# Hybrid decoder layer on one core: the values of head group A projected token-major ahead of attention, and pairs of 12 units instead of 16

## The reference

```
def dilated_attention(q, k, v, slopes):            # group A
    for window, d in ((128, 1), (512, 4), (2048, 16)):
        num, m, sm = banded_parts(every d-th token of q, k, v, slopes, window // d, d)
    w = [exp(m_i - max of m)]                      # the three branches are merged
    return sum(num_i * w_i) / sum(s_i * w_i)
def swa_sink_attention(q, k, v, slopes, sinks):    # group B: window of 128, a sink in the denominator
    return (num * c) / (s * c + exp(sink - m2))

mix = concat(rmsnorm(out_a, g_a), rmsnorm(out_b, g_b))
x = x + mix @ w_out
h = rmsnorm(x, ffn_norm)
x = x + (silu(h @ w_gate) * (h @ w_up)) @ w_down   # inner width 5632
return rmsnorm(x, final_norm)
```

## Time and profile before

| | |
|---|---|
| time, median of 3 runs | 1996.04 us (1995.95 to 1996.41) |
| time of the profiled execution | 1995.92 us |
| span of its trace | 1994.1 us |
| PE busy | 1984.3 us, 10380 matmuls |
| DVE, ACT, POOL busy | 1612.9, 1091.5, 145.6 us |
| one pair with attention (359.4 to 416.5 us of the span) | 57.1 us: DVE 37.0, ACT 31.7, POOL 14.1 us busy |

### The profile page before, as it was taken

How to read it: one execution, slowest core, us unless ns; L and a number is a source line. 1 busy time by engine, 2 the same in 40 slices (tenths; PEclk the granted TensorE clock), 3 DMA queues, 4 the chain that set the end, 5 groups by cost and what they waited for, 6 DMA issues and landing times.

```text
span 1994.1 us, 30321 instructions
## 1 busy us (share of the span) xinstructions
PE 1984.3 (100%) x10380; PEld 1703.7 (85%) x10380; DVE 1612.9 (81%) x2319; ACT 1091.5 (55%) x2001; POOL 145.6 (7%) x241
## 2 busy tenths in 40 slices
PE   9999999999999999999999999999999999999998
PEld 8888888888888998888888888888888888888886
DVE  5666667666766899999999999999999688697876
ACT  6455556556435655555555555555456355566643
POOL 1122222222100000000000000000000000000000
PEclk9999999999999999999999999999999999999999
DMA  8222222223434344434443444443446846546343
GB/s 300 85 75 70 78 74 75 73 69 92 146 99 141 131 140 136 138 128 137 137 137 129 141 133 136 137 134 130 137 137 221 314 130 210 181 149 225 123 131 133
DMA packets 131899, 273.88 MB, mean 137 GB/s; under 512 B 13568, under 2 KB 13600, under 8 KB 130768
## 3 DMA queue, kind: packets, MB, share of 16 engines
q1 hardware_dynamic: 119344, 233.36, 37.0%
q0 software_dynamic: 6640, 23.82, 3.0%
q10 hardware_dynamic: 5808, 15.23, 2.1%
HBM read 240.89 MB, written 31.46 MB: 137 GB/s over the span
## 4 chain that ended last, share of the span: by engine, by line
PE 99%; issue 0%; DMA 0%; DVE 0%; ACT 0%; SPq 0%; POOLq 0%; POOL 0%
PE bank L686 27%; PE bank L689 14%; PE bank L569 8%; PE bank L571 7%; PE bank L570 7%; PE bank L613 7%; PE bank L615 7%; PE bank L614 7%; PE bank L745 3%; PE bank L743 3%; PE bank L744 3%; PE bank L770 2%; PE bank L787 1%; PE bank L755 1%; PE bank L754 1%; PE bank L786 1%
## 5 line engine op out<-in xcount | busy, mean ns | idle before, releaser
L686 PE MATMUL bank<-s_two,t_hi 128*128 128x512 f32 x2352 | 557.4, 391 | 0.0
L686 PEld LDWEIGHTS bank<-s_two,t_hi 128*128 128x128 f32 x2352 | 433.6, 188 | 84.6
L1199 ACT ACTIVATE t_hi<-t_raw 128x1792 fp32r<-128x1792 f32 x176 | 302.6, 1721 | 361.1 <-DVE t_raw L1774 275.4
L1497 DVE TENSOR_TENSOR w_lo<-raw,w_hi 128x512 fp32r<-128x512 f32 x300 | 208.4, 696 | 212.6 <-ACT w_hi L972 210.8
L1780 DVE TENSOR_TENSOR t_lo<-t_raw,t_hi 128x1792 fp32r<-128x1792 f32 x176 | 355.3, 2019 | 19.1 <-ACT t_hi L1199 18.9
L972 ACT ACTIVATE w_hi<-raw 128x512 fp32r<-128x512 f32 x300 | 188.2, 629 | 265.5 <-PE bank L615 144.6
L689 PEld LDWEIGHTS bank<-s_two,t_lo 128*128 128x128 f32 x2352 | 298.9, 191 | 10.2 <-DVE t_lo L1780 0.2
L689 PE MATMUL bank<-s_two,t_lo 128*128 128x256 f32 x2352 | 302.3, 283 | 0.0
L1771 DVE TENSOR_TENSOR t_raw<-t_raw 128x1024 f32<-128x1024 f32 x176 | 214.7, 1220 | 18.3 <-DMA t_raw<-in_w_gu 16.1
L569 PE MATMUL bank<-h_hi,w_hi 128*128 128x512 f32 x544 | 218.8, 402 | 1.0 <-DVE h_lo L1501 1.0
L571 PE MATMUL bank<-h_lo,w_hi 128*128 128x512 f32 x544 | 213.3, 392 | 0.0
(11 more groups left out here) (216 smaller groups left out, 3119.6 us busy)
## 6 DMA issues: line engine op xcount, KB each, us to landing
t_raw<-in_w_gu SPq DMA_DIRECT2D x348, 256.0 KB, 2.7
raw<-in_w_in SPq DMA_DIRECT2D x136, 256.0 KB, 2.6
raw<-in_w_down SPq DMA_DIRECT2D x112, 256.0 KB, 3.6
gu_mid<-part POOLq DMA_DIRECT2D x43, 512.0 KB, 2.9
gu_next<-gu_mid SPq DMA_DIRECT2D x36, 512.0 KB, 6.8
raw<-in_w_out SPq DMA_DIRECT2D x64, 256.0 KB, 3.1
fast_y<-in_w_down SPq DMA_DIRECT2D x24, 512.0 KB, 5.0
fast_z<-in_w_down SPq DMA_DIRECT2D x16, 512.0 KB, 4.4
```

Source lines behind the costliest of these rows:

```text
L686: mm = nc.tensor.matmul(b[:, :], t_hi[r][:, ti, q, :], both, start=d == 0 and q == 0, stop=d == DOUBLES - 1 and q == 1 and i < 4, skip_gro ...
L1199: nc.scalar.activation(t_hi[r][:, :, :, :].rearrange("p a q c -> p (a q c)"), t_raw[r][:, 1:8, :, :].rearrange("p a q c -> p (a q c)"), AC ...
L1497: nc.vector.tensor_tensor(w_lo[:, s, :], raw[:, s, :], w_hi[:, s, :].bitcast(F32), ALU.subtract).then_inc(w_lo_done, 1)
```

## The change

The values of A leave the pairs. They are projected in two groups of eight heads (16 units each) ahead of attention, with the activations stationary and the weights moving, so that the result lies token-major; ACT takes each group from four banks, scales it by the tokens' inverse norm and leaves it in a part of `o_t` which the output of the same pair overwrites later. The turn of A's values, its bank use and its `take` are gone; the pair's two halves of values are made from `o_t`. The early stage is now: 16 units of values, the 12 units of pair 0, 16 units of values.

A pair has 12 units (queries of A, keys of A, queries of B). Attention still has 16 steps: the last four (12 to 15), and the output and squares of the fourth head (now steps 16 and 17), stand in the first steps of the next pair, each ahead of the attention of the new pair. B's `q_high` and `q_low` move from step 1 to step 2. The pairs are written out, not looped; the halves of B's second key and value head come in steps 3 and 5 of pair 5, and the first four splits of attention output (`act_high`, `act_low`), which stood between the last pair and the output projection, in steps 2, 5, 8 and 11 of pair 7. POOL scales the first head's rows ahead of adding the squares of the pair before.

```
-U_PAIR = 8
-U_OUT = U_PAIR + 16 * PAIRS
+U_V = (8, 36)
+U_FIRST = 24
+U_PAIR = 52
+PAIR_U = 12
+U_OUT = U_PAIR + PAIR_U * (PAIRS - 1)
-BANK_Q, BANK_K, BANK_V = 0, 1, 4
+BANK_Q, BANK_K, BANK_QB = 0, 4, 1
+BANK_VA = ((0, 4, 6, 1), (5, 7, 4, 6))
...
@@ PE @@
+        def v_unit(n, k):
+            unit = U_V[n] + k
+            pe.wait_ge(w_lo_done, unit + 1)
...
+            for t in range(NT):
+                mm = wide_products(t, bank[BANK_VA[n][t]], h_hi[:, k, :], h_lo[:, k, :], k, unit % 4, k == 0, k == KD - 1)
...
         def attend(s, a):
...
-            if s == 2:
-                pe.wait_ge(acc_taken, 5 + 4 * a)
...
-                turn_v().then_inc(vt_ready, 1)
...
+        def attend_both(s, a):
+            if a > 0 and s + PAIR_U < 16:
+                attend(s + PAIR_U, a - 1)
+            attend(s, a)
...
+        def pair(p):
+            for c, b in enumerate((BANK_Q, BANK_K, BANK_QB)):
...
+                for j in range(4):
+                    tall_unit(u_pair(p) // 4 + c, j, b, h_hi, h_lo)
+                    attend_both(4 * c + j, p - 1)
...
@@ ACT @@
         def attend(s, a):
-            if s == 0 and not (isinstance(a, int) and a == 0):
-                o_lower(a - 1, 3)
-            if s == 1 and not (isinstance(a, int) and a == 0):
-                o_square(a - 1, 1)
+            if s == 16:
+                o_lower(a, 3)
+            if s == 17:
+                o_square(a, 1)
...
             if s == 3:
-                act.wait_ge(vt_ready, a + 1)
-                nc.scalar.activation(v_both["A"][:, :, 0:4:3, :], bank[BANK_O][:, :]...
+                act.wait_ge(v_taken, NT * (kv_of(a) + 1))
+                if a > 0:
+                    act.wait_ge(pv_done, ROUNDS * a - 4)
+                nc.scalar.activation(v_both["A"][:, :, 0:4:3, :], o_t[:, a, :]...
...
+        def attend_both(s, a):
+            if a > 0 and s < 18 - PAIR_U:
+                attend(s + PAIR_U, a - 1)
+            attend(s, a)
+
+        def v_take(n):
...
+            for t in range(NT):
...
+                nc.scalar.activation(o_t[:, 4 * n:4 * n + 4, P * t:P * (t + 1)], bank[BANK_VA[n][t]]...,
+                                     ACT.Copy, scale=inv[:, t:t + 1]).then_inc(v_taken, 1)
+
+        def pair(p):
+            a = p - 1
+            for s in range(PAIR_U):
+                split(*ahead_of(u_pair(p) + s))
+                attend_both(s, a)
+                if p == 1 and s == 0:
+                    v_take(1)
+                if s == 2:
+                    q_high("B", proj[1], 3 * p + 2, qb_hi_done)
                 if s == 5:
                     act.wait_ge(s_ready, 16 * a + 8)
+                    q_high("A", proj[0], 3 * p + 3, qa_hi_done)
...
+                if a == 4 and s == 3:
+                    kb_high(1)
+                if a == 4 and s == 5:
+                    vb_high(1)
+                if p == PAIRS - 1 and s in (2, 5, 8, 11):
...
+                    act_high(0, (s - 2) // 3)
...
@@ DVE @@
         def attend(s, a):
+            if s == 16:
+                take_o(a, 3)
             if s == 0:
-                if not (isinstance(a, int) and a == 0):
-                    take_o(a - 1, 3)
                 set_bias(a, 0)
...
+        def pair(p):
+            u, a = u_pair(p), p - 1
+            for s in range(PAIR_U):
+                split(*ahead_of(u + s))
                 if s == 0:
                     dve.wait_ge(ka_hi_done, 4 * p)
                     dve.wait_ge(ka_lo_done, 2 * p)
-                    take(proj[1][:, :], BANK_K, -0.125, u)
+                    take(proj[1][:, :], BANK_QB, -0.125, u)
                 if s == 8:
                     take(proj[1][:, :], BANK_K, 1.0, u + 8)
-                attend(s, a)
-                if s == 1:
+                attend_both(s, a)
+                if s == 2:
                     q_low("B", proj[1], qb_hi_done, 2 * p, qb_lo_done)
...
-                if s == 12:
-                    take(proj[0][:, :], BANK_V, 1.0, u + 12)
+                if a == 4 and s == 3:
+                    kb_low(1)
+                if a == 4 and s == 5:
+                    vb_low(1)
+                if p == PAIRS - 1 and s in (2, 5, 8, 11):
+                    act_low(0, (s - 2) // 3)
...
@@ DVE, output projection @@
-                        take(proj[1][:, :], BANK_K, -0.125, U_OUT)
-                    attend(s, PAIRS - 1)
+                        take(proj[1][:, :], BANK_QB, -0.125, U_OUT)
+                    attend_both(s, PAIRS - 1)
@@ POOL @@
         def attend(a):
+            scale_rows(a, 0)
             if not (isinstance(a, int) and a == 0):
                 add_squares(a - 1, 1)
-            scale_rows(a, 0)
```

More of the change, by code:

```diff
@@ L795, in turn_v, with attend @@
             return mm
-        def attend(s, a, kv):
-            first = isinstance(a, int) and a == 0
+        def attend(s, a):
+            kv = kv_of(a)
             if s == 0:
@@ L803, in attend @@
                 pe.wait_ge(ka_hi_done, 4 * (a + 1))
-                if first:
+                if a == 0:
                     pe.wait_ge(k_rest_zero, 4)
-                if not first:
+                else:
                     pe.wait_ge(exp_done, 16 * a)
@@ L890, in _ @@
             first_unit(m)
[L891 to L896, removed]
+        early()
+        for p in range(1, PAIRS):
+            pair(p)
         for g in range(2):
@@ L1005, in exps @@
             kind = HEAD[h][0]
-            if i0 == 0 and not (isinstance(a, int) and a == 0 and h < 2):
+            if i0 == 0 and not (a == 0 and h < 2):
                 act.wait_ge(pt_ready, ROUNDS * a + (-2, 0, 3, 6)[h])
@@ L1120, in square_row, with early @@
             nc.scalar.activation(x_row[t][:, :], x_row[t][:, :], ACT.Square, accum_out=sums[:, t, 0:1]).then_inc(sq_done, 1)
-        def pair_0():
-            for s in range(16):
-                split(*ahead(U_PAIR // 4 + s // 4, s % 4))
+        def early():
+            for s in range(U_PAIR - U_V[0]):
+                split(*ahead_of(U_V[0] + s))
                 if s == 0:
@@ L1643, in k_lower, with attend_both @@
                          4 * p + h + 1, ka_lo_done)
-        def pair(p, a):
-            u = U_PAIR + 16 * p
-            for s in range(16):
-                split(*ahead(U_PAIR // 4 + 4 * p + s // 4, s % 4))
+        def attend_both(s, a):
+            if a > 0 and s < 17 - PAIR_U:
+                attend(s + PAIR_U, a - 1)
+            attend(s, a)
+        def pair(p):
+            u, a = u_pair(p), p - 1
+            for s in range(PAIR_U):
+                split(*ahead_of(u + s))
                 if s == 0:
@@ L1724, in act_low @@
                                            hi[:, k, :].bitcast(F32), ALU.mult, ALU.subtract).then_inc(act_lo_done, 1)
+        early()
+        dve.wait_ge(consts_loaded, 16 * 5)
+        nc.vector.tensor_scalar(neg_sink[:, :], sink[:, :], -1.0, None, ALU.mult).then_inc(neg_done, 1)
+        dve.wait_ge(neg_done, 1)
+        for p in range(1, PAIRS):
+            pair(p)
         def add_out(g, n):
```

211 lines of the change are left out of this document (112 added, 99 removed).

## The result

The changed kernel takes 2002.96 us (median of 6 runs, 2002.32 to 2003.73) against 1996.09 us (1995.61 to 1996.41) for the kernel before, run on the same chip: ratio 1.0034, with a 95% interval from 1.0023 to 1.0044. It is slower by 6.9 us. The profiled execution took 2002.93 us with a span of 2001.1 us. The whole loss lies in the attention stage: the first unit of the output projection starts at 473.6 us in the trace of before and at 477.5 us in the one after, the seventeenth (the first with no attention beside it) at 531.0 and at 538.0 us, 7.0 us later, and nothing is lost or won behind that.

What follows compares the result with a forecast made beforehand. The prediction took PE to bound the kernel, so only less PE work or late results count. From 1995.9 us, 13.2 us of new waits against 3.6 us less work gave 2005.5 us, range 1996.0 to 2011.0.

Steps and rivals of the forecast that it cites:

- The turns: Eight turns of A's values leave PE, 0.44 us each: 3.6 us less work.
- Step 12, now beside step 0: DVE's take of B's queries delays the third head's low half; PE waits 0.56 us seven times, 3.9 us.
- Steps 5 and 6: The first head's two rounds come late for PE: 0.82 us in each of six pairs, 4.9 us.
- 0.62 pass on: In step 5 the squares delay ACT's chain by their full 0.62 us; against 0.30 cover, PE stalls 0.32 us.
- The lateness of the second head's minima: DVE brings them later in step 4, up to 1.0 us more a pair; half of that taken.
- Step 3: PE's weighing of the fourth head waits for DVE's backlog: 0.1 us a time, seven times, put at 0.8 us.
- Pair 5: Halves of B's second keys and values in steps 3 and 5 make PE wait 2.0 us, bounds 0 and 2.6.
- Pair 7: Halves of attention output joining steps 2 and 5 make PE wait 1.0 us, bounds 0 to 1.3.
- The output projection: Beside it ACT copies a group of four banks in step 3: 0.6 us of waits, bounds 0 to 0.8.
- all stays covered: Rival: queue order does not matter and only the turns count, 1992.3 us; chance 13%.
- Only the two tight chains: Rival: only step 12 and steps 5 and 6 stall, by lower bounds, +2.2 us, 1998.1 us; chance 22%.
- the backlog doesn't clear: Rival: DVE's work is too much for the shorter pairs, all upper bounds hold, 2011 us; chance 10%.

Runs made afterwards that it cites:

- e3: The kernel before, with each of the eight turns of A's values done twice into the same bank: 1999.33 us, ratio 1.0018.
- e4: The kernel before, with DVE taking the values ahead of step 12's attention instead of behind it: 2000.22 us, ratio 1.0021.
- e9: The kernel before, with the fourth head's squares on ACT in step 5 and POOL scaling the first head's rows ahead of adding squares: 1997.12 us, ratio 1.0007.
- e10: The changed kernel, with the fourth head's squares on ACT in step 4 instead of step 5: 2000.54 us, ratio 1.0023 to the kernel before.
- e5: The changed kernel, in pairs 2 to 7: B's queries taken behind step 0's attention, squares in step 4, halves of B's queries in step 1: 1993.29 us.
- e8: The changed kernel, with only the extra work of pairs 5 and 7 moved to steps 10 and 11 of pairs 4 to 7: 1998.70 us.
- e6: The changed kernel with the edits of e5 and the move of single pairs' work of e8: 1991.09 us, ratio 0.9977 to the kernel before.
- e1: The changed kernel, with DVE's take of B's queries behind step 0's attention, also in the output projection: 2001.53 us, ratio 1.0028 to the kernel before.
- e2: The changed kernel, with the fourth head's squares on ACT behind step 6's second high half: 2002.90 us, ratio 1.0036 to the kernel before.
- e7: The kernel before, with the fourth head's squares on ACT in step 5 instead of step 1, POOL's order unchanged: 2047.27 us, ratio 1.0258.

## Why the prediction was right, and where its terms were not

The forecast was 2005.5 us, slower by 9.6, from 13.2 us of new waits less 3.6 us of work; measured were 6.9 us. The mechanism is as it was put: DVE's and ACT's results come late for PE in the named steps while both have idle time. Of its steps:

- *The turns*, 3.6 us: 3.5 by e3. Right; 8 x 0.44 is 3.5, as 7 x 0.1 in step 3 is 0.7 and not 0.8, and the two slips cancel in the sum.
- *Step 12, now beside step 0*, 7 x 0.56 = 3.9: 0.60 in each of the seven places, 4.2 by the trace, with the take between the split and the denominators. Right; e4 brings the same loss (4.4) into the kernel before by that order alone. The 0.04 too few are the weight load, which stood as the upper bound.
- *Steps 5 and 6*, 4.9: too high. Measured are 6 x 0.44 = 2.6 us, and they lie in step 6 alone. The term "0.62 pass on" failed: a queue moves by the distance of the starts, 0.52, and 0.11 of that is absorbed, so the part of the squares is 0.16 (e9) and not 0.32. The lateness of the second head's minima was put at 0.5 and is 0.28, the rest of 0.44; and the two stall PE only together, since e10, without the squares in step 5, has no wait there in a plain pair.
- *Step 3*, 0.8: measured 0.15 to 0.19 in each of seven places, 1.2 us. e5's halves of B's queries in step 1 take it away.
- *Pair 5*, 2.0: 2.6 by the length of the pair, some 0.2 of which the kernel before had too. *Pair 7*, 1.0: 1.7. Both together 4.2 by e8. Of the bounds given, pair 5 came to the upper end, as was argued, and pair 7 above its own of 1.3: of the four splits of the output, those of steps 2 and 5 come just ahead of the waits in steps 3 and 6, where no cover was left, and the turn in step 9 (469.64), behind the split of step 8, waits 0.24 us too.
- *The output projection*, 0.6: 0.1.
- *Missed*: in step 4 of pair 1 the turn waits 0.45 us for POOL's rows, a place that the prediction did not name; with the halves of B's queries in step 1 (e5) that wait is gone. Against it, units with no attention beside them run faster by 1.9 us in all, and 0.45 us of waits that the kernel before had in pair 5 and at the start of the output projection are gone.

The measured sum is 4.2 + 2.6 + 1.2 + 2.6 + 1.7 + 0.1 + 0.45 = 12.85 us of waits, less 3.5, 1.9 and 0.45: +7.0 us, which is the difference of the spans (2001.1 - 1994.1). So the 13.2 us of new waits were nearly right as a sum, but by errors that cancel: 2.3 too many in steps 5 and 6, 1.9 too few in all others. What the forecast is too high by is mostly the 1.9 us of the faster units.

Of the rivals, *all stays covered* is wrong as a forecast, but its 1992.3 us is near where the kernel gets when the order is mended (e6, 1991.1, with the faster units that the rival did not count). *Only the two tight chains* (1998.1) comes near what is left when the work of pairs 5 and 7 is moved (e8, 1998.7), in part by luck: e8 also holds the waits of step 3 and of pair 1, against the faster units. That *the backlog doesn't clear* is refuted by e6 and e10. Not settled: what makes PE's starts 0.0034 us farther apart beside attention, and how the 0.28 us of step 6 divide among the instructions that the short pair adds to DVE in steps 2 to 4; no run took one of them out alone.

## What to carry to other kernels

When two stages are laid over each other, don't compare sums of busy time: list for each result that the bound engine needs the end of its producer against the start of its consumer, and put the edit's new instructions behind the one with the least cover in each queue. What has no consumer near (a take, squares, splits for a later stage) goes to the steps with no such chain, but ask first which bank or which other engine's queue it holds up, as e1, e2 and e7 show. A move that is free in the queue where it is made can cost in the next one.

## What the runs showed of the hardware that was not expected

- A 512-column matmul with its own weight load starts 0.2267 us after the one before when nothing else uses PE between the units, and 0.2294 to 0.2301 us where attention stands beside them, at the same granted clock of 1.00 (before and after).
- Independent instructions in a row on ACT overlap: the start distance is 0.52 us for lengths of 0.62 (e9), and DVE's is 0.60 for 0.69 (step 0 after). In these places an added instruction moved its queue by the former.
- A wait of PE costs 0.05 to 0.06 us more than the time for which it is late, in each place of step 0 and step 6, because a weight load is no longer hidden: in step 6 of pair 6 the turn's own load starts with it, at 409.59, where without a wait (e6) it starts 0.23 us ahead, and the second turn follows after 0.16 instead of 0.11 us. PE goes on 0.06 us after DVE's end.
- A DVE instruction of 0.58 us (TENSOR_SCALAR, 128x256) took 1.22 beside POOL's addition of two tensors (e2), and 0.58 beside POOL's scaling of rows (after, at 409.45).
